# 128 bytes of padding in the on-chip layout of a one-core, two-block transformer kernel

## The reference

```python
def swiglu(x, w_gu, w_d):
    gate, up = jnp.split(x @ w_gu, 2, axis=-1)
    return (jax.nn.silu(gate) * up) @ w_d
...
x = x + 0.5 * rms_norm_2(swiglu(rms_norm_2(x, g[0]), ffn_wgu[i, 0], ffn_wd[i, 0]), g[1])
h = rms_norm_2(x, g[2])
...                                   # mix = the mixer of layer i
x = x + rms_norm_2(mix, g[3])
x = x + 0.5 * rms_norm_2(swiglu(rms_norm_2(x, g[4]), ffn_wgu[i, 1], ffn_wd[i, 1]), g[5])
```

## Time and profile before

| | |
|---|---|
| median of three runs | 3111.27 us |
| the profiled execution | 3112.57 us |
| its span | 3110.8 us |
| PE busy | 3023.7 us, 97% |
| PEld busy | 2567.9 us, 83% |
| DVE busy | 2130.3 us, 68% |
| ACT busy | 1527.0 us, 49% |
| mean granted PE clock | 0.991 |

### The profile page before, as it was taken

How to read it: one execution, slowest core, us unless ns; L and a number is a source line. 1 busy time by engine, 2 the same in 40 slices (tenths; PEclk the granted TensorE clock), 3 DMA queues, 4 the chain that set the end, 5 groups by cost and what they waited for, 6 DMA issues and landing times.

```text
span 3110.8 us, 49298 instructions
## 1 busy us (share of the span) xinstructions
PE 3023.7 (97%) x19037; PEld 2567.9 (83%) x19037; DVE 2130.3 (68%) x3065; ACT 1527.0 (49%) x2263; POOL 67.2 (2%) x115
## 2 busy tenths in 40 slices
PE   7999999899999999998999999999999999999998
PEld 3888887788779897767878989789988787779996
DVE  5576666899878586775578867786864443588685
ACT  4454645677645354563245534554543332455452
POOL 1000000000000000300000000000000000000000
PEclk9999999899999999999999999999999999999999
DMA  5222222799823232210013323232222222223221
GB/s 225 89 76 79 76 81 83 274 379 380 318 70 121 95 109 86 68 56 18 24 61 108 109 96 108 82 122 102 102 95 83 80 82 81 75 76 121 102 102 68
DMA packets 97101, 354.81 MB, mean 114 GB/s; under 512 B 10896, under 2 KB 11280, under 8 KB 96528
## 3 DMA queue, kind: packets, MB, share of 16 engines
q1 hardware_dynamic: 92448, 334.54, 30.5%
q0 software_dynamic: 3168, 11.54, 1.0%
q10 hardware_dynamic: 1296, 6.11, 0.5%
HBM read 344.27 MB, written 7.86 MB: 113 GB/s over the span
## 4 chain that ended last, share of the span: by engine, by line
PE 89%; DVE 5%; ACT 4%; issue 1%; DMA 1%; POOL 0%; SPq 0%; ACTq 0%; DVEq 0%; POOLq 0%
PE bank L353 13%; PE bank L355 13%; PE bank L354 13%; PE bank L961 7%; PE bank L963 7%; PE bank L962 7%; PE bank L2812 2%; PE bank L2814 2%; PE bank L2813 2%; PE bank L557 1%; PE bank L558 1%; PE bank L562 1%; PE cbank L379 1%; PE bank L3969 1%; PE gbank L1646 1%
## 5 line engine op out<-in xcount | busy, mean ns | idle before, releaser
L325 ACT ACTIVATE whi<-raw 128x1024 fp32r<-128x1024 f32 x310 | 319.2, 1050 | 219.5 <-PE bank L355 182.4
L344 DVE TENSOR_TENSOR wlo<-raw,whi 128x1024 fp32r<-128x1024 f32 x310 | 375.5, 1222 | 71.1 <-ACT whi L325 70.3
L353 PE MATMUL bank<-h_hi_buf,whi 128*128 128x512 f32 x1008 | 409.7, 406 | 8.2 <-DVE h_lo_buf L493 5.1
L355 PE MATMUL bank<-h_hi_buf,wlo 128*128 128x512 f32 x1008 | 394.5, 391 | 0.0
L354 PE MATMUL bank<-h_lo_buf,whi 128*128 128x512 f32 x1008 | 394.0, 391 | 0.0
L353 PE MATMUL bank<-a_hi_buf,whi 128*128 128x512 f32 x832 | 324.9, 391 | 0.5 <-DVE wlo L344 0.5
L354 PE MATMUL bank<-a_lo_buf,whi 128*128 128x512 f32 x832 | 323.8, 389 | 0.0
L355 PE MATMUL bank<-a_hi_buf,wlo 128*128 128x512 f32 x832 | 323.7, 389 | 0.0
L353 PEld LDWEIGHTS bank<-h_hi_buf,whi 128*128 128x128 f32 x1008 | 189.9, 188 | 54.7 <-DVE h_lo_buf L493 6.8
L355 PEld LDWEIGHTS bank<-h_hi_buf,wlo 128*128 128x128 f32 x1008 | 189.7, 188 | 41.3
L354 PEld LDWEIGHTS bank<-h_lo_buf,whi 128*128 128x128 f32 x1008 | 190.1, 189 | 40.1 <-issue 4.1
(11 more groups left out here) (724 smaller groups left out, 7251.9 us busy)
## 6 DMA issues: line engine op xcount, KB each, us to landing
raw<-in_w SPq DMA_DIRECT2D x622, 512.0 KB, 4.4
held<-in_w SPq DMA_DIRECT2D x12, 512.0 KB, 16.5
x<-in_x ACTq DMA_DIRECT2D x2, 2048.0 KB, 11.1
sorted_y<-ysb POOLq DMA_DIRECT2D x6, 512.0 KB, 7.7
token_rows<-hrow POOLq DMA_DIRECT2D x4, 512.0 KB, 4.3
out<-x SPq DMA_DIRECT2D x8, 256.0 KB, 2.0
xc<-in_xc ACTq DMA_DIRECT2D x1, 1024.0 KB, 8.7
sorted_y<-zrow POOLq DMA_DIRECT2D x1, 512.0 KB, 3.1
```

The source lines that it names most:

```text
L325: act.activation(weights(k, g)[0], k.raw[:, g.slot, :], ACT.Copy).then_inc(k.split_hi, 2 * RING + 1 if first == COND_GROUPS * RING else 1)
L344: dve.tensor_tensor(lo, k.raw[:, g.slot, :], hi.bitcast(F32), ALU.subtract).then_inc(k.split_lo, 2 * RING + 1 if first == COND_GROUPS * RI ...
L353: pe.matmul(out, w_hi, hi, start=(t == 0), stop=False)
L355: return pe.matmul(out, w_lo, hi, start=False, stop=(t == tiles - 1))
```

## The change

A gap of 128 bytes is put between `h_lo_buf` and `a_hi_buf`. All that lies behind it, and all that is laid over what lies behind it, moves up by 128 bytes; `raw`, `whi`, `wlo`, the h buffers and what lies over them stay. The diff also adds a helper that nothing calls. The instructions of every engine, their order and their waits are the same; only addresses differ.

```diff
+        def both_halves_behind(name, shape, names, skew):
+            n = int(np.prod(shape[1:]))
+            begin = at
+            t = bump(name, [P, 2 * n + skew // 4], F32R)
...
+            return cut(0), cut(1)
         k.ones = bump("ones", [P, P])
...
         k.h_hi_buf = bump("h_hi_buf", [P, DC, T], F32R)
         k.h_lo_buf = bump("h_lo_buf", [P, DC, T], F32R)
+        at += 128
         k.a_hi_buf = bump("a_hi_buf", [P, DC, T], F32R)
         k.a_lo_buf = bump("a_lo_buf", [P, DC, T], F32R)
```

More of the change, by code:

```diff
@@ L4810, in bump @@
             return t
+        def both_halves_behind(name, shape, names, skew):
+            n = int(np.prod(shape[1:]))
+            begin = at
+            t = bump(name, [P, 2 * n + skew // 4], F32R)
+            for b, half in enumerate(names):
+                arena[half] = (begin + 4 * n * b, begin + 4 * n * (b + 1))
+            cut = lambda b: t[:, skew // 4 + b * n:skew // 4 + (b + 1) * n].rearrange("p (c f) -> p c f", c=shape[1])
+            return cut(0), cut(1)
         k.ones = bump("ones", [P, P])
```

## The result

The kernel got slower by 0.4%: a median of 3126.86 us in six runs (3122.93 to 3127.76), against 3112.44 us for the kernel before in six runs (3108.00 to 3118.02). The ratio is 1.0043, with a 95% interval of 1.0030 to 1.0056: about +14 us, where I had forecast -37. The profiled execution has a span of 3126.0 us instead of 3110.8, +15.2.

What follows compares the result with a forecast made beforehand. PE was taken to bound the kernel, carrying 89% of the chain of waits. A gain of 6 ns on each of 6195 matmuls, 37.2 us, off 3112.6 gave 3075 us, range 3040 to 3145.

Steps and rivals of the forecast that it cites:

- The 13 ns: Overhead per fp32r matmul beside a weight load, read as two reads colliding; at most 11.2 ns to be had back.
- the retention's 2 ns: Plain fp32 matmuls of the retention pay only 2 ns each beside a weight load, so 13 ns is no fixed price.
- The split by distance: Only matmuls whose two operands move apart change, 3123 long and 3072 short; forms keeping their distance stay at 389 and 283.
- I take 6 ns for every one of the 6195: Gain assumed for every matmul moved apart, from the smallest overhead seen (283 - 277): 37.2 us in all.
- the 3072: Matmuls of 256 columns moved apart, mixes past weights and h past sums; 6 ns gain each, at most 27.6 us together.
- the 3123 long ones: Matmuls of 512 columns moved apart, mostly a past weights; 6 ns gain each, at most 35.0 us together.
- the bound of 31 us: Loss if shifted matmuls act like `hc`: 9 ns on each long one, 28 us, and 1 ns on short ones, 3 us.
- Rival 2: Shifted operands collide more, as in `hc` long ones: slower, from a few us up to 3144 us and beyond; chance 0.24.
- both doors of it: Weights move up in "s1", "s4" and parked blocks, the moving side elsewhere; one may gain and the other lose.
- Rival 1: Distance between operands doesn't matter: 3112 us, 3108 to 3116; chance 0.30.
- `c4`: Stationary operand off the grid; its 384-column matmuls average 336 ns as interpolated, so a shift of 16 to 112 bytes does nothing.
- Rival 3: All of the 13 ns goes in the shifted products: 3050 us, or 3042 with expert stage and `hc`; chance 0.15.

Runs made afterwards that it cites:

- `pad256`: 256 bytes of padding in front of the a buffers instead of the change's 128; median 3113.13 us against 3114.08 for the kernel before, ratio 1.0000.
- `micro_forms`: Matmuls alone, no computation: hi/lo pattern of three, alternating widths, other types and widths at several distances; pattern of three 226.7 ns at 0, 233.4 at 32 bytes.
- `micro_seven`: Matmuls alone: the seven products in kernel order at 64 pairs of sums and mixes offsets; 120.0 ns a matmul at (0, 0), 117.1 to 117.2 at the best.
- `micro_distance`: Matmuls alone, fp32r, 48 address pairs, 512, 256 and 384 columns; by distance modulo 256 bytes, 226.7 to 234.3 ns (512), 113.4 to 120.0 (256).
- `sums64_mixes192`: Kernel before with the sums buffers 64 bytes off and the mixes 192, a buffers unmoved; median 3099.06 us against 3114.27, ratio 0.9949.

## Why the prediction was wrong

**The bound: right.** PE carried the chain, nanoseconds on a matmul came through to the span (+15.8 by forms, +15.2 in the span), and no wait appeared. DVE and DMA were no part of it: `pad256` moves the same buffers and costs nothing, and with the 128 bytes DVE is busy 1.5 us longer in 3126 and ACT 0.5, so the edits that I costed at nothing were rightly costed. The expert stage wasn't as far from PE as I held when I left it out of the sum: from 560 to 880 us the kernel after falls behind by 2.0 us.

**The 13 ns: shown in part.** For fp32r the cost depends on the addresses of the two reads together, and for plain fp32 and bf16 it doesn't, as the retention's 2 ns had said; `micro_forms` has 2.5 ns for bf16 too. That all of the 13 ns is collision isn't shown: no run has an fp32r matmul without its weight load, 320 columns pay 13.3 ns at all four distances tried, and no distance takes more than 6.7 ns off (256 columns, where the pace of the load, 112 ns, leaves room for 8). In the Trainium skill, TensorE: Matmul & The Clock Gate, section "Step-by-step: what each phase is for", the two read ports are independent and a load takes nothing from the running matmul. The bf16 and fp32 rows agree with it. The fp32r rows don't: with nothing but PE at work, the same 512 columns take 226.7 or 233.4 ns by the distance of the two operands alone. The measurement decides.

**The split by distance: half right.** The long forms that kept their distance stayed (227.9 and 227.8 ns). The short ones did not (120.0 to 119.1 and 119.9 to 119.4): the rhythm of a stream outlasts the product that set it, as `micro_seven` shows with PE alone.

**The step that failed** is "I take 6 ns for every one of the 6195". One sign and one size were put on both widths. Measured, the 2496 lost 6.5 ns each, +16.1 us, and the 3072 won 1.3 each, -3.9. The terms of the sum were -18.7 us for the 3123 long ones and -18.4 for the short ones; they came out as about +19 and -4, with +2.5 of the expert stage and -2 of the neighbours beside them. The reason that I gave for a gain was that 13 ns looked like a full collision, from which every other distance could only lead away. For 256 columns that is so: 0 is the worst of the eight distances. For 512 it is the best, and no row that I read of before said so.

**The evidence that I had, and luck.** `hc` showed the long form at 398 and the short one down to 277: dearer long ones and cheaper short ones, in one stream, by 9 and 6 ns, where the change brought 6.5 and 1.3. That the signs are alike is luck. `hc` lies at distance 0 in the kernel before, and `micro_forms` has the same picture at distance 0 (230.0 and 116.6 ns), so it comes from alternating the two widths. Moved by 128 bytes, `hc` went the other way: by starts its long ones went from 234.8 to 230.8 ns and its short ones from 116.5 to 118.0. It was no witness for another distance, and the bound of 31 us that I drew from it held by chance.

**The rivals.** Rival 2, more collision, had the right mechanism on the long forms, both doors of it (a past weights +6.5, h past parked blocks +4.8 ns), and 31 us where it was +15, because the short ones gained instead of losing 1 ns. Rival 1, that distance doesn't matter, is out. Its argument that the two reads meet in all pieces of the memory at any starting distance doesn't hold: the starting distance alone moves the pace by up to 7.6 ns at 512 columns. Its witness `c4` was read by durations, and a nanosecond or three can't be seen in a mean of 336 that is held against an interpolated one. With the weights 16 to 112 bytes up, its distances are 144 to 240, where the table has 174.1 to 176.7 ns at 384 columns against 173.3 at 0. By the starts in the trace of before its gaps vary from 168 to 179 ns, where a steady stream at distance 0 has 173 or 174, and their mean is 173.2 to 173.5 in each of its eight passes, no more than at distance 0. Each of its tiles stands at another distance and its column is read with step zero; no run takes these apart, so it stays open why `c4` doesn't pay. Rival 3 is out: the best gap found, 113.4 ns for 256 columns, keeps 6.7 of the 13.3.

**What stays open.** What in the memory has a period of 256 bytes, why 32 and 96 bytes are dear at 512 columns and 64 hardly is, what the rhythms are, and whether the part that no distance removes is collision at all. The runs give the table, not its cause.

## What to carry to other kernels

A cost that is the same to the nanosecond in all forms can be a property of the one layout that all share; before a buffer is moved, a kernel of nothing but the matmuls in question, with a line for each distance and for each width, gives the whole table in one run, and the sign may differ between widths. Move only the operands of the forms that gain, and leave those of 512 columns at a distance of a multiple of 256 bytes. Measure the real order of the products too, since a table of single forms overrates or underrates the mixture (113.4 became 115.1 and 116.8, 117.8 became 115.5 and 115.9), while the small kernel with the real order gave every product to 1 ns in 1400.

## What the runs showed of the hardware that was not expected

- An fp32r matmul with its weight load takes, over one column in 0.417 ns, 13.3 ns at distance 0 for 256, 384 and 512 columns. By the distance of moving operand and weights modulo 256 bytes it is 13.3 to 21 (512 columns), 13.3 to 16.7 (384) or 6.7 to 13.3 ns (256). At the four distances tried 320 columns always take 146.7 ns, 192 and 128 always 112, and 448 take 200.0 to 204.0, the least at 64 bytes (`micro_distance`, `micro_forms`).
- bf16 takes 215.8, 109.2 and 55.9 ns for 512, 256 and 128 columns with a weight load each, and plain fp32 429.2 ns for each of its two instructions of 512, at all distances tried (`micro_forms`).
- The same 12 matmuls at the same addresses take 1.36 or 1.39 us, by the products in front of them (`sums64_mixes192`).
